# A causal mask moved from TensorE to VectorE: a minimum of the exponentials in place of a mask product

## The reference

```python
s = (jnp.einsum('bqhd,bshd->bhqs', qn, k_nope)
     + jnp.einsum('bqhd,bsd->bhqs', qp, k_pe)).astype(jnp.float32)
s = jnp.where(k_pos[None, :] <= q_pos[:, None], s, NEG_INF)
p = jax.nn.softmax(s, axis=-1).astype(v.dtype)
return jnp.einsum('bhqs,bshd->bqhd', p, v)
```

## Time and profile before

| | us |
|---|---|
| median of 3 runs | 3318.26 |
| lowest and highest run | 3317.94 and 3321.26 |
| the profiled execution | 3319.38 |
| its span, first to last instruction of the program | 3317.6 |
| the eight pairs of the second attention, in the trace | from 1586.8 to 2519.7 |

### The profile page before, as it was taken

The page is one execution under the profiler, slowest core; times in us unless marked ns, Lnnn a source line. Parts: engine busy times, 40 slices in busy tenths (PEclk is TensorE's granted clock), DMA queues, the critical chain, the costliest instruction groups (busy, mean ns, idle before and its releaser), DMA issues. The chain is left out here.

```text
span 3317.6 us, 57379 instructions
## 1 busy us (share of the span) xinstructions
PE 3020.5 (91%) x19987; PEld 2372.6 (72%) x19987; DVE 1701.9 (51%) x4096; ACT 1226.0 (37%) x2624; POOL 1814.9 (55%) x1482
## 2 busy tenths in 40 slices
PE   7999986996999996997999999999998996999992
PEld 5677754885988885996656666666665885888881
DVE  3666665774443333553545555655562663444333
ACT  3444543221232333443434444444442221333323
POOL 3666652443344432444698889888873222444444
PEclk9999988997999998999799999999998997999996
DMA  3111115543999984655320221122013544999976
GB/s 112 47 55 55 55 56 177 180 151 125 336 319 315 319 257 99 165 158 136 99 52 14 55 53 28 40 55 52 11 61 113 197 146 168 329 322 312 317 234 222
DMA packets 246954, 497.29 MB, mean 150 GB/s; under 512 B 88477, under 2 KB 165745, under 8 KB 219496
## 3 DMA queue, kind: packets, MB, share of 16 engines
q1 hardware_dynamic: 213448, 418.40, 38.0%
q0 software_dynamic: 33312, 76.43, 9.8%
HBM read 367.28 MB, written 136.21 MB: 152 GB/s over the span
## 5 line engine op out<-in xcount | busy, mean ns | idle before, releaser
L2205 POOL TENSOR_TENSOR keep_wg<-keep_wg,ab_pT 128x1024 f32<-128x1024 f32 (+2 forms) x320 | 597.4, 1867 | 91.8 <-ACT ab_pT L2239 50.0
L2239 ACT ACTIVATE ab_pT<-ab_S 128x512 f32<-128x512 f32 (+4 forms) x704 | 349.9, 505 | 514.9 <-PE ab_S L2337 250.6
L1357 POOL DMA_INDIRECT scratch_h<-ex_y,ex_prow x65 | 118.2, 1819 | 449.7 <-issue 203.7
L2266 DVE TENSOR_REDUCE ab_mx<-ab_W 128x2 f32<-128x800 f32 (+1 forms) x224 | 249.7, 1117 | 210.3 <-PE ab_W L2351 205.7
L1529 PE MATMUL ex_G<-ex_xT,keep_wg 128*128 128x160 f32 x2080 | 297.3, 302 | 10.8 <-DMA ex_wu<-in_moe_w_up 10.8
L1529 PEld LDWEIGHTS ex_G<-ex_xT,keep_wg 128*128 128x128 f32 x2080 | 288.1, 192 | 12.2 <-DMA ex_wu<-in_moe_w_up 11.4
L1529 PE MATMUL ex_U<-ex_xT,ex_wu 128*128 128x160 f32 x2080 | 293.1, 299 | 0.0
L1529 PEld LDWEIGHTS ex_U<-ex_xT,ex_wu 128*128 128x128 f32 x2080 | 286.1, 190 | 0.0
L2386 PE MATMUL ab_O<-ab_pT,keep_wg 128*64 128x512 f32 (+4 forms) x1408 | 265.2, 518 | 0.0
L1402 DVE TENSOR_TENSOR ex_wd_lo<-ex_wd,ex_wd_hi 128x2048 fp32r<-128x2048 f32 x65 | 149.0, 2292 | 159.8 <-ACT ex_wd_hi L1395 159.8
L386 POOL TENSOR_TENSOR aa_work<-aa_work,aa_rden 128x1088 f32<-128x1088 f32 x68 | 134.6, 2001 | 132.3 <-DVE aa_rden L548 132.3
(11 more groups left out here) (333 smaller groups left out, 7721.4 us busy)
## 6 DMA issues: line engine op xcount, KB each, us to landing
keep_wg<-in_moe_w_gate SPq DMA_DIRECT2D x65, 1024.0 KB, 7.8
ex_wu<-in_moe_w_up SPq DMA_DIRECT2D x65, 1024.0 KB, 13.9
ex_wd<-in_moe_w_down SPq DMA_DIRECT2D x65, 1024.0 KB, 14.4
scratch_h<-pr_h SPq DMA_DIRECT2D x33, 512.0 KB, 5.3
scratch_xn<-pr_xn SPq DMA_DIRECT2D x33, 512.0 KB, 2.9
pr_o<-scratch_oT SPq DMA_DIRECT2D x32, 512.0 KB, 5.0
scratch_qT<-pb_qT SPq DMA_DIRECT2D x17, 768.0 KB, 5.2
scratch_oT<-keep_wg SPq DMA_DIRECT2D x17, 512.0 KB, 2.8
```

The source lines that it names most:

```text
L2205: nc.gpsimd.tensor_tensor(to, to, pT[:, U % RING, :, 0:n], ALU.add).then_inc(added, 1)
L2239: nc.scalar.activation(pT[:, U % RING, h, 0:n], S[:, h, 0:n], ACT.Exp, scale=B_SCALE).then_inc(exped, 1)
L2266: nc.vector.reduce_max(mx[:, :, t, c:c + 1].rearrange("p h a -> p (h a)"), W[:, j % 2, :, 0:n], AX.X).then_inc(emptied, 1)
```

## The change

The fourth product of PE on the diagonal units goes, and with it the tensors `identb` and `maskT`. In its place DVE takes the minimum of pT and a new float32 tensor `most`, which is 3e38 where a position counts and 0 where it is masked. It is done in place, in the masked columns, for both heads in one instruction. A new semaphore `cut` counts these instructions; POOL's add and PE's attend of a diagonal unit wait for it and no longer for the exponentials. DVE does the minimum of unit U - 1 at the head of its step U, ahead of the jobs of this step.

```diff
-                sp.dma_start(identb[:, :], io["identb"]).then_inc(consts, 16)
                 sp.dma_start(mask[:, :], io["mask_b"]).then_inc(masks_in, 16)
+                sp.dma_start(most[:, :], io["most_b"]).then_inc(masks_in, 16)
                 sp.dma_start(ident[:, :], io["ident"]).then_inc(consts, 16)
-                sp.dma_start(maskT[:, :], io["mask_bT"]).then_inc(consts, 16)
...
                 def add(U):
-                    pool.wait_ge(exped, 2 * U + 2)
+                    if U in cuts:
+                        pool.wait_ge(cut, cuts[U])
+                    else:
+                        pool.wait_ge(exped, 2 * U + 2)
...
-                dve.wait_ge(masks_in, 16)
+                dve.wait_ge(masks_in, 32)
...
+                def cut_off(U):
+                    tri = masked(U)
+                    n = tri.stop - tri.start
+                    dve.wait_ge(exped, 2 * U + 2)
+                    nc.vector.tensor_tensor(pT[:, U % RING, :, 0:n], pT[:, U % RING, :, 0:n],
+                                            most[:, tri].unsqueeze(1).to_broadcast([P, 2, n]), ALU.min).then_inc(cut, 1)
+
                 for U in range(-1, NU + 8):
+                    if U - 1 in cuts:
+                        cut_off(U - 1)
                     for job in work[U]:
...
-                        last = nc.tensor.matmul(to, k_lo[p % 2][0:QD, h, kb], q_hi[p % 2][0:QD, h, qs], start=False, stop=not diagonal)
-                        if diagonal:
-                            last = nc.tensor.matmul(S[:, h, 0:tri.stop - tri.start], identb[:, :], maskT[:, tri], start=False, stop=True)
+                        last = nc.tensor.matmul(to, k_lo[p % 2][0:QD, h, kb], q_hi[p % 2][0:QD, h, qs], start=False, stop=True)
...
                     if (p, g) == (0, 0):
-                        pe.wait_ge(consts, 16 * 3)
+                        pe.wait_ge(consts, 16)
...
                 def attend(U):
-                    pe.wait_ge(exped, 2 * U + 2)
+                    if U in cuts:
+                        pe.wait_ge(cut, cuts[U])
+                    else:
+                        pe.wait_ge(exped, 2 * U + 2)
```

More of the change, by code:

```diff
@@ L1986, in attention_b @@
     closes = {(p, g): U for U, (p, g, b) in enumerate(units)}
+    diagonal = [U for U, (p, g, b) in enumerate(units) if b >= 4 * g]
+    cuts = {U: k + 1 for k, U in enumerate(diagonal)}
     scans = []
@@ L2016, in attention_b @@
         ident = s.sb("ident", [P, P])
-        identb = s.sb("identb", [P, P], BF16)
         mask = s.sb("mask", [P, 512])
         junk = s.sb("junk", [P, 2, 2, 512], BF16)
-        maskT = s.sb("maskT", [P, P + META], BF16)
+        most = s.sb("most", [P, P + META])
         ones = s.sb("ones", [P, HD])
@@ L2054, in attention_b @@
         scored = s.sem("scored")
+        cut = s.sem("cut")
         exped = s.sem("exped")
@@ L2319, in score @@
                     p, g, b = units[U]
-                    n, kb, tri = width(U), keys(U), masked(U)
+                    n, kb = width(U), keys(U)
                     at = P * (4 * g + 5) - n
@@ L2329, in score @@
                             pe.wait_ge(moved[g], 32 * moves(p, g))
-                    diagonal = b >= 4 * g
                     for h in range(2):
@@ L2653, in shape_constants @@
         "ident": np.eye(P, dtype=np.float32),
-        "identb": np.eye(P).astype(bf),
         "cs_a": table(HD),
@@ L2658, in shape_constants @@
         "mask_b": np.concatenate([np.zeros((P, 512 - P)), np.where(k <= q, 0, MASKED)], axis=1).astype(np.float32),
-        "mask_bT": np.concatenate([np.where(q <= k, 0, MASKED), np.where((q >= P - META) & (q - (P - META) <= k), 0, MASKED)[:, 0:META]], axis=1).astype(bf),
+        "most_b": np.concatenate([np.where(q <= k, 3e38, 0), np.where((q >= P - META) & (q - (P - META) <= k), 3e38, 0)[:, 0:META]], axis=1).astype(np.float32),
         "ones_tri": np.concatenate([(q < k).astype(np.float32), np.ones((P, P), np.float32)], axis=1).astype(bf),
```

## The result

The changed kernel takes 3338.4 us in the median (3334.35 to 3340.47, 5 runs) against 3319.13 (3317.94 to 3321.26, 5 runs) of the kernel before on the same chip: a ratio of 1.0054, 95% interval 1.0040 to 1.0067, so +19.3 us. Its profiled execution took 3339.64 us with a span of 3337.8.

A forecast was written before the change was run, and what follows sets the result against it. PE was taken to pace the outer pairs, with PE and POOL both close in middle ones. Six middle pairs at +3.0 (+18) and two outer at -3 (-6) gave +12: 3318.3 to 3330 us; forecast 3325 to 3345, full range 3303 to 3365.

The forecast's parts named there:

- Part 1, the relief: Removing 320 mask products saves PE 3.2 us a pair; first and last pairs were to gain 3 us each.
- Part 2, the exclusion: DVE minimums and POOL adds exclude each other: 0.1 us of POOL per minimum, 1.4 us a middle pair; minimums wait 1.2.
- Part 2, the place in the queue: Minimums queued behind DVE's divide steps delay POOL's adds at units 3 and 11; 1.6 us paid per middle pair.
- the walk: Step-by-step trace of queue delays: POOL's unit 11 add 3.1 us late, unit 16 add 1.6 us late.
- the +3.0 predicted for each middle pair: Each of six middle pairs slower: 1.6 us from queue place plus 1.4 us from port exclusion.
- DVE falls behind in the masked stretches: Rival: PE waits for DVE's scans around pair boundaries, 5 us at each of seven places, +35, 3365 us; chance 0.21.
- The exclusion costs nothing: Rival: minimums beside POOL's adds cost no port time; +4 in six pairs, less 6, 3317 us; chance 0.20.
- PE's relief lands: Rival: POOL's adds not late at units 3 and 11; middle pairs gain 11 us, outer 6, 3301 us; chance 0.17.
- Part 3, the loads: Two small loads go and one comes at kernel start: put at nothing, 0.5 us either way.

The follow-up runs named there:

- one-input run: Changed kernel with mask products kept and each minimum replaced by a maximum reading one tensor, same columns, waits and queue place: 3333.4 us, ratio 1.0044 to the kernel before.
- the relief alone: Changed kernel without its minimums, so no mask product either, diagonal exponentials taken with scale 0: whole 3721.0 us (later stage altered), second-attention stage 937.2 us.
- the kernel before with its last pair edited: Kernel before with the output weights' split begun at the 24th unit of the last pair instead of the 6th: 3322.3 us, ratio 1.0007.

## Why the prediction was right or wrong

**Direction and size.** Slower, as forecast: +19.3 us for a predicted +12. 3338.4 lies in the forecast's own 3325 to 3345. But in part that was luck, for the sum came near by terms that erred in both directions: the six middle pairs cost 12.9 us for a predicted 18, and the two outer ones 4.3 us together for a predicted gain of 6.

**Part 1, the relief.** The size was about right: PE's busy time in a pair at full clock fell by 2.4 us for a predicted 3.2. Of "I take 3 us in each" the first pair bears out the size, 3.4 us between the means of seven profiles and seven, but it comes with a clock that rises sooner, of which the sum knows nothing. In the last pair it was +10.6 in place of -3. In the middle pairs PE stands longer at the divide in place of finishing earlier, and the clock falls behind many of these stands, a price that appears nowhere in the sum.

**Part 2, the exclusion.** That it exists and makes the minimum wait was right. Two sizes were off. I took 1.2 us of waiting on average; the minimums lasted 0.91 us and the one-input operations in their place 0.36, so that they waited some 0.5. And I took 0.1 us of POOL's time for each minimum in the stretch where POOL is never idle, 1.4 us in a pair. In the fifth pair the stretch from the add of unit 16 to the pair's last add, with ten minimums, takes 78.15 us against 77.92: 0.2 us, where I had 1.0. Those that wait for an add end within 0.3 us of its end, in POOL's gap before the next. So most of the 18 us that the second input costs went through DVE instead, by what is queued behind the minimum, over half of it in the last pair.

**Part 2, the place in the queue.** The links of the walk were right. These rows answer to the earlier trace rows, fourth pair, POOL at units 3 and 11, then DVE:

```profile
1971.13 0.80 POOL L2210 TENSOR_TENSOR keep_wg<-keep_wg,ab_pT 128x288 f32<-128x288 f32 x1 [2.37 <-DVE ab_pT L2307]
...
1991.21 1.35 POOL L2210 TENSOR_TENSOR keep_wg<-keep_wg,ab_pT 128x544 f32<-128x544 f32 x1 [2.19 <-DVE ab_pT L2307]
```

```profile
1984.39 1.23 DVE L2307 TENSOR_TENSOR ab_pT<-ab_pT,ab_most 128x256 f32<-128x256 f32 x1
1985.54 1.21 DVE L2271 TENSOR_REDUCE ab_mx<-ab_W 128x2 f32<-128x1024 f32 x1
1986.68 3.34 DVE L2299 RECIPROCAL keep_wg<-ab_W 128x512 f32<-128x512 f32 x1
1990.11 0.69 DVE L2301 TENSOR_TENSOR ab_o<-ab_O,keep_wg 128x512 f32<-128x512 f32 x1
1990.72 0.41 DVE L2307 TENSOR_TENSOR ab_pT<-ab_pT,ab_most 128x256 f32<-128x256 f32 x1
```

Minimum, scan, reciprocal, product, minimum, add: as the walk has it. Its sizes have to be read in POOL's own time, for PE no longer stands where it stood: in the fifth pair POOL's first add comes 1.58 us less behind PE's first score than before (7.20 against 8.78), and PE reaches unit 11 1.6 us earlier (25.33 against 26.97). Counted from PE's first score of the fifth pair, the add of unit 11 is only 0.85 us late. Counted from POOL's first add it is 2.4 us late (25.75 against 23.33), where the walk had 3.1, and the add of unit 16 1.0 us (35.58 against 34.56), where it had 1.6. With the 0.2 us behind unit 16 POOL loses 1.24 us in the pair, and these come out as PE's longer stand at the next divide. That is the walk's 3.0 us, mis-sized: 1.24, with 1.2 of the difference in the 14 minimums behind unit 16.

So the +3.0 predicted for each middle pair, +2.15 measured on average, was near the truth with half of its reason missing. Of the 2.9 us from divide to divide in the sixth and the seventh pair 1.2 are the delay that the walk followed, and 1.7 are the low clock behind PE's stand, which I didn't give.

**The last pair and the first rival.** The rival "DVE falls behind in the masked stretches" named the mechanism that made the last pair 10.6 us longer, and in the middle pairs it is there in the small: PE waits for the maximum 7.1 us in its matmuls and 7.9 for scans. It overrated the waits (0.5 us where 0.7 was its bound) and so gave +35. My sum had nothing for it, though the earlier trace rows shows the subtractions of the last pair waiting for the same adds: I read them for the price of the exclusion and not as work that would meet the minimums there. That is the mis-sized term: -3 for +10.6.

**The other rivals.** "The exclusion costs nothing" fell with the one-input run (18 us). "PE's relief lands" fell for the middle pairs: with the relief alone five of the six were longer than before, and their sum was 7.4 us longer.

**Part 3, the loads.** Nothing, within the spread: the stage began between 1586.5 and 1594.4 us in the thirteen other profiled runs, with the loads in either order.

**Left open.** Why the clock falls at one stand and not at another is not settled, and the length of the stand doesn't decide it. In the kernel before with its last pair edited, PE stood 1.71 us at the first divide of the fourth pair and 1.73 at that of the fifth:

```profile
1960.58 1.08 PE L2374 MATMUL ab_W<-keep_wg,ab_ones 128*64 128x512 f32 x4 [1.71 <-POOL keep_wg L2205]
1961.49 3.97 PE L2386 MATMUL ab_O<-ab_pT,keep_wg 128*64 128x16 f32 x16
...
2075.25 1.08 PE L2374 MATMUL ab_W<-keep_wg,ab_ones 128*64 128x512 f32 x4 [1.73 <-POOL keep_wg L2205]
```

Behind the first the clock fell (0.72 in the 6 us from 1960.0), behind the second it stayed at 1.00. With the one-input operation 2.24 us left it at 1.00 in the third pair and not in the fourth, and in the changed kernel it fell at 2068.2 behind a stand of 1.38 us for a scan. So the number of falls doesn't follow from the lengths of the stands, and each profile is one execution. Nor was it tried what the changed kernel takes with the clock held up.

## What to carry to other kernels

When work moves from TensorE to VectorE, ask first what TensorE stands for at its next wait: if it is another engine, the time given back is standing time, and standing can cost the clock on top (some 1.7 us for a fall here). An operation with two SBUF inputs, placed where GpSimd adds without a pause, should be counted in VectorE's queue with its wait and everything behind it, and with the other operations there that wait for the same adds; doing it once with a one-input stand-in in the same place tells the port from the queue. Before relieving an engine, double the work in question and look at the stretches at full clock: here twice the mask products cost 0.5 to 1.5 us of a middle pair where the sum had 3.2, and the engine to relieve was GpSimd (8 us). And measure a pair of a repeating stage from wait to wait: between PE's first scores the fifth pair had lost nothing, between its divides 1.2 us.

## What the hardware showed that I had not expected

The granted clock falls at short stands of TensorE, and not at all of them. With stands of 2.10 and 2.39 us TensorE went to 1.2 GHz; sixteen attends took 3.69 and 3.99 us in place of 2.27. From its second pair on the stage had 10.2 us of low clock before, 47.8 after the change, 58.6 with less work on TensorE and nothing added, and 6.8 with the mask product doubled (10.2 and 6.8 differ by a single fall, which says nothing; the other two lie far outside the 6.8 to 13.7 of the four profiles with mask products, nothing of the change and the divides in place).

At the stage's start it is the reverse: the clock rises 9.9 to 10.4 us after it in the seven kernels without the bf16 mask products, and 17.6 to 31.2 us after it in the seven with them.

GpSimd's adds are hardly slowed by short two-input operations of VectorE (0.2 us in a stretch of 78 with ten of them), while a long one cost an add 0.89 us. In the middle pairs the cost is nearly all VectorE's: its 256 columns went from 0.41 to 1.01 us.
